# Expert loop in another order: the next expert's gate and up products ahead of the present expert's down products

## Chip, cores and metric

One NeuronCore of a Trainium2 chip runs the whole program. The metric is the device time of one execution in microseconds (us), median of the runs. All data is 32-bit float.

## What is computed

One step of a decoder of two layers over 512 prompt tokens and 32 sample tokens (544 in all). Each layer is an attention stage (latent attention in layer 0, sliding window in layer 1) followed by a mixture of experts: 32 experts, each token goes to 2 of them. Cut to what matters here:

```
def run_block(args):                      # rows of one expert, weights of that expert
    xb, e = args
    hid = jax.nn.silu(xb @ w_gate[e]) * (xb @ w_up[e])      # 1024 -> 512, twice
    return hid @ w_down[e]                                  # 512 -> 1024
...
yr = yr.astype(jnp.float32) * row_w[:, None]
y = jnp.zeros((n_tok, shape[-1]), jnp.float32).at[row_tok].add(yr)
```

The weights of an expert are three matrices of 2 MiB (gate, up, down), so 32 experts in two layers read 64 x 6 MiB from memory.

## The kernel before, in words

The kernel is written by hand for each engine; nothing plans the order, semaphores alone tie the engines together. `happened(name, k)` is "the event `name` has come k times", `landed` the same for a transfer. Each layer has a function `experts(L)` on every engine, with a loop over the 32 experts e; b is the parity of e (which of two buffers), s = (e + 2) % 3 the weight slot.

What one expert e does:

- TensorE (`expert`, L2320 to L2354): *gate and up*, 16 matmuls of 512 columns in pairs that share the array (64 columns of it each), from xeT[b] and the slot's gate and up weights into PSUM bank b, signal gu_mm; `fetched_T(e + 1)`, 8 transposes of the next expert's gathered rows (signal xt_mm); `numbers(e + LOOK)`, five small matmuls that give the row numbers of expert e + 3 (idx_mm); the wait for the hidden rows (hid_ready) and 4 transposes of them (ht_mm); the wait for hidT_ready, and *down*, 8 matmuls of 512 columns in pairs into bank 2 + b (d_mm).
- ScalarE (L974 to L983): after gu_mm, Silu from bank b; `rows_T(e + 1)`, the copy of the transposed rows to xeT; after d_mm, the copy of one half of the result to ye[b] (y0_ready).
- VectorE (L1575 to L1593): `mark(e + 3)`, the product silu x up (L1582, hid_ready), `numbers(e + 3)` (L1524, L1526), the copy of the transposed hidden rows to hidT (L1587), the copy of the other half of the result (L1593).
- GpSimd: gathers the rows of expert e + 3 from memory (L664), scatters the result rows of e (L674).
- SyncE issues the weight transfers (L495 to L500) and has three slots for them. Expert e's gate and up (L487) go out once gu_mm of e - 3 has come, its down (L492) once d_mm of e - 3 has come, strictly in this order on one queue.

In the trace all matmuls carry the line of the helper `mm` (L1923) and all transposes that of `flip` (L1928). The trace joins a run of matmuls that follow each other: "x48" is the 16 pieces of one expert's down and the 32 of the next one's gate and up (each 32-bit matmul shows as two pieces).

After the loop of layer 0 SyncE loads the projection weights of layer 1 (wqkv): 4 MiB after gate and up of expert 30 (L528), 2 MiB after its down (L530). After either loop the result rows are read back (L547).

Of the kernel before, what the change touches and what calls it, by code (L numbers as in the profile page):

```python
# [13 lines left out]
D = 1024  # L14
# [158 lines left out]
def build(nc, a, o):  # L173
    with ExitStack() as ctx:
# [556 lines left out]
        def _(act):  # L731
            start_counts(act, "scalar")

            def copy(out, in_):
                return act.activation(out, in_, ACT.Copy)  # L735
# [207 lines left out]
            def experts(L):  # L943
# [30 lines left out]
                with act.Fori(0, NE // 2) as i:  # L974
                    for b in range(2):
                        e = 2 * i + b
                        act.wait_ge(sig["gu_mm"], happened("gu_mm", NE * L + e + 1))
                        act.wait_ge(sig["hid_ready"], happened("hid_ready", NE * L + e))
                        act.activation(sg[BLK:2 * BLK, :], ps[0:BLK, b, :], ACT.Silu).then_inc(sig["silu_ready"], 1)  # L979
                        rows_T(e + 1, 1 - b)  # L980
                        act.wait_ge(sig["d_mm"], happened("d_mm", NE * L + e + 1))
                        act.wait_ge(sig[f"scattered{b}"], landed(f"scattered{b}", STORES * L + i + 1))
                        copy(ye[b][0:BLK, 0:FF], ps[0:BLK, 2 + b, :]).then_inc(sig["y0_ready"], 1)  # L983
# [124 lines left out]
        def _(v):  # L1108
# [358 lines left out]
            def experts(L):  # L1467
# [107 lines left out]
                with v.Fori(0, NE // 2) as i:  # L1575
                    for b in range(2):
                        e = 2 * i + b
                        v.wait_ge(sig["idx_mm"], happened("idx_mm", FETCHES * L + e + LOOK - 1))
                        mark(e + LOOK, 1 - b)
                        v.wait_ge(sig["silu_ready"], happened("silu_ready", NE * L + e + 1))  # L1580
                        v.wait_ge(sig["ht_mm"], happened("ht_mm", NE * L + e))
                        v.tensor_tensor(hid[0:BLK, :], sg[BLK:2 * BLK, :], ps[BLK:2 * BLK, b, :], ALU.mult  # L1582
                                        ).then_inc(sig["hid_ready"], 1)
                        numbers(e + LOOK, 1 - b)
                        v.wait_ge(sig["ht_mm"], happened("ht_mm", NE * L + e + 1))
                        v.wait_ge(sig["d_mm"], happened("d_mm", NE * L + e))
                        v.tensor_copy(hidT, ps[:, 6, 0:KF * BLK].rearrange("p (k t) -> p k t", k=KF)  # L1587
                                      ).then_inc(sig["hidT_ready"], 1)
                        v.wait_ge(sig[f"scattered{b}"], landed(f"scattered{b}", STORES * L + i + 1))
                        v.tensor_copy(store_at[b][0:BLK, :], store_rows[0:BLK, cols(e, 1)])  # L1590
                        v.drain()
                        v.wait_ge(sig["d_mm"], happened("d_mm", NE * L + e + 1))
                        v.tensor_copy(ye[b][0:BLK, FF:D], ps[BLK:2 * BLK, 2 + b, :]).then_inc(sig["y1_ready"], 1)  # L1593
# [325 lines left out]
        def _(pe):  # L1919
# [341 lines left out]
            def experts(L):  # L2261
# [58 lines left out]
                def expert(i, r):  # L2320

                    e, b, s = 6 * i + r, r % 2, (r + 2) % SLOTS
                    pair, turn = 3 * i + r // 2, LOADS[(r + 2) % SLOTS] * L + 2 * i + r // SLOTS + 1
# [11 lines left out]
                    fetched_T(e + 1, 1 - b, (odd if b == 0 else even) + pair + 1)  # L2335
# [7 lines left out]
                    last.then_inc(sig["ht_mm"], 1)  # L2343
# [12 lines left out]
                with pe.Fori(0, NE // 6) as i:  # L2356
                    for r in range(6):
                        expert(i, r)
                for r in range(NE % 6):
                    expert(NE // 6, r)  # L2360
# [340 lines left out]
```

## Time and profile before

| what | us |
|---|---|
| median of 3 runs | 1859.22 |
| lowest and highest run | 1856.38, 1862.15 |
| the profiled execution, its own time | 1855.08 |
| span of the profiled execution | 1853.4 |
| mean granted TensorE clock in it, share of full speed | 0.931 |

The profiled execution is 4.1 us below the median of the runs. The expert loop of layer 0 runs from about 517 to 1020 us of the span, that of layer 1 from about 1316 to 1819 us, so that the two loops are more than half of the time. All times in the rows are us from the start of the span.

### The profile page before, as it was taken

How to read it: one execution, taken by the hardware profiler on the slowest of the kernel's cores; microseconds unless marked ns; L12 is line 12 of the kernel's file. 1: busy time of each engine (PE TensorE's matmuls, PEld its weight loads, DVE VectorE, ACT ScalarE, POOL GpSimd, SP SyncE). 2: the span in 40 equal slices, each digit the busy share in tenths (PEclk: the TensorE clock that was granted, in tenths of full speed). 3: DMA queues.
4: the chain of work that ended last, by engine and by line, in shares of the span. 5: the costliest groups of instructions: out<-in, count | busy, mean ns of one | idle time of the engine just before them, and what ended most of it. 6: DMA issues, size and time to landing. Idle time of an engine off the chain costs nothing.

```text
span 1853.4 us, 27694 instructions
## 1 busy us (share of the span) xinstructions
PE 1672.0 (90%) x9306; PEld 874.9 (47%) x9307; DVE 541.4 (29%) x1490; ACT 420.5 (23%) x888; POOL 247.8 (13%) x348
## 2 busy tenths in 40 slices
PE   7899899999888989898889999899898989899885
PEld 5466666655544444444434445455443434344332
DVE  2333343322421111111111656764211111111113
ACT  2233344421111111111111224341011111111112
POOL 1231024400011111111111301000111111111110
PEclk9899899999888999998999999999798989898987
DMA  5252137744489999999998800122999999999973
GB/s 180 70 153 85 50 128 251 250 160 164 172 339 405 409 411 408 405 410 408 411 411 362 308 13 6 41 112 108 360 399 412 415 412 405 403 403 406 404 329 150
DMA packets 83342, 515.60 MB, mean 278 GB/s; under 512 B 22664, under 2 KB 41049, under 8 KB 56794
## 3 DMA queue, kind: packets, MB, share of 16 engines
q1 hardware_dynamic: 61962, 461.35, 62.7%
q0 software_dynamic: 21296, 53.15, 8.7%
q8 instruction: 50, 0.82, 0.2%
q14 instruction: 34, 0.28, 0.0%
HBM read 506.99 MB, written 26.52 MB: 288 GB/s over the span
## 4 chain that ended last, share of the span: by engine, by line
PE 76%; DMA 7%; issue 6%; DVE 6%; ACT 3%; DVEq 1%; SPq 0%; ACTq 0%; POOLq 0%
PE ps L1923 67%; PE ps L1928 9%; DMA mem<-in_moe_w_up 5%; DVE mem L1582 1%; ACT mem L979 1%; ACT mem L735 1%; DMA mem<-moe_rows_back 1%; DVE mem L1701 0%; DMA mem<-in_cache_mla 0%; DMA mem<-in_mla_w_a 0%; DMA moe_rows_back<-mem 0%; DVE mem L1293 0%; ACT mem L906 0%; ACT mem L909 0%; DVE mem L1672 0%
## 5 line engine op out<-in xcount | busy, mean ns | idle before, releaser
L1923 PE MATMUL ps<-mem 128*64 128x512 f32 (+13 forms) x7330 | 1433.9, 493 | 100.3 <-issue 49.7
L1923 PEld LDWEIGHTS ps<-mem 128*64 128x64 f32 (+4 forms) x7330 | 646.1, 150 | 797.3 <-issue 710.4
L735 ACT ACTIVATE mem<-ps 128x512 f32<-128x512 f32 (+3 forms) x370 | 205.8, 568 | 723.0 <-PE ps L1923 526.3
L1928 PE MATMUL ps<-mem 128*128 128x128 f32 (+1 forms) x1976 | 273.4, 280 | 73.6 <-DVE mem L1582 45.7
L1928 PEld LDWEIGHTS ps<-mem 128*128 128x128 f32 (+1 forms) x1976 | 233.8, 171 | 172.6 <-issue 149.5
L1582 DVE TENSOR_TENSOR mem<-mem,ps 64x512 f32<-64x512 f32 x64 | 44.2, 690 | 471.0 <-ACT mem L979 471.0
L664 POOL DMA_INDIRECT mem<-moe_rows_in,mem x68 | 63.3, 931 | 559.6 <-issue 541.4
L1593 DVE COPY mem<-ps 64x512 f32<-64x512 f32 x64 | 44.4, 693 | 312.3 <-PE ps L1923 312.3
L674 POOL DMA_INDIRECT moe_rows_back<-mem x64 | 59.2, 925 | 355.0 <-DVE mem L1593 347.8
L979 ACT ACT_TABLE_LOAD x32 | 41.1, 1283 | 231.8 <-PE ps L1923 231.8
L979 ACT ACTIVATE mem<-ps 64x512 f32<-64x512 f32 x64 | 37.7, 589 | 199.8 <-PE ps L1923 199.4
L1281 DVE COPY mem<-ps 128x512 f32<-128x512 f32 x64 | 44.2, 692 | 77.3 <-PE ps L1928 73.2
L625 POOL DMA_DIRECT2D mem<-in_cache_mla x96 | 51.5, 537 | 104.8 <-PE ps L1923 94.8
L605 POOL DMA_DIRECT2D mem<-in_cache_mla x64 | 34.7, 542 | 114.3 <-issue 114.3
L1019 ACT ACTIVATE mem<-mem 128x256 f32<-128x256 f32 (+1 forms) x64 | 30.3, 474 | 61.8 <-DVEq L1706 61.8
L646 POOL DMA_DIRECT2D moe_rows_in<-mem x10 | 5.4, 537 | 239.1 <-DVE mem L1409 239.1
L1587 DVE COPY mem<-ps 128x256 f32<-128x256 f32 x64 | 27.2, 425 | 24.6 <-PE ps L1928 20.4
L1701 DVE CUSTOM_DVE_ANT_0 mem<-ps,mem 128x256 f32<-128x256 f32 (+1 forms) x64 | 26.3, 448 | 27.2 <-PE ps L1923 25.1
L1517 DVE TENSOR_TENSOR mem<-mem 128x320 f32<-128x320 f32 x70 | 33.7, 481 | 1.5 <-issue 0.7
L850 ACT ACTIVATE mem<-mem 128x128 f32<-128x128 f32 (+3 forms) x32 | 18.0, 561 | 37.7 <-DVEq L1230 37.7
L1627 DVE SCALAR_TENSOR_TENSOR mem<-mem 128x1024 f32<-128x1024 f32 (+1 forms) x16 | 20.5, 1281 | 20.4 <-DMA mem<-moe_rows_back 19.6
L752 ACT ACTIVATE mem<-mem 128x1024 f32<-128x1024 f32 x10 | 10.6, 1057 | 65.7 <-DVEq L1374 53.6
(233 smaller groups left out, 459.8 us busy)
## 6 DMA issues: line engine op xcount, KB each, us to landing
mem<-in_moe_w_gate SPq DMA_DIRECT2D x64, 2048.0 KB, 17.8
mem<-in_moe_w_up SPq DMA_DIRECT2D x64, 2048.0 KB, 25.5
mem<-in_moe_w_down SPq DMA_DIRECT2D x64, 2048.0 KB, 23.5
mem<-in_cache_mla POOLq DMA_DIRECT2D x160, 160.0 KB, 4.5
mem<-in_cache_mla SPq DMA_DIRECT2D x96, 160.0 KB, 5.5
mem<-moe_rows_back SPq DMA_DIRECT2D x8, 1024.0 KB, 8.3
mem<-in_mla_wo SPq DMA_DIRECT2D x1, 4096.0 KB, 14.2
moe_rows_in<-mem POOLq DMA_DIRECT2D x8, 512.0 KB, 3.0
```

The costliest lines, as they stand in the source:

```text
L605: g.dma_start(pages_flat[par][:, bass.ds(j * ROW, ROW)], a["cache_mla"][0][bass.ds(page, 1)].rearrange("a p c -> p (a c)")).then_inc(sig[f ...
L625: g.dma_start(pages[b % 2][:, j, :], a["cache_mla"][0][bass.ds(at[n], 1)].rearrange("a p c -> p (a c)")).then_inc(sig[f"late_pages{b % 2}" ...
L664: g.indirect_dma_start(out=xe[b][0:BLK, :], out_offset=None, in_=rows_in, in_offset=bass.IndirectOffsetOnAxis(ap=fetch_at[b][0:BLK, 0:1].b ...
L674: g.indirect_dma_start(out=rows_back, out_offset=bass.IndirectOffsetOnAxis(ap=store_at[b][0:BLK, 0:1].bitcast(U32), axis=0), in_=ye[b][0:B ...
L735: return act.activation(out, in_, ACT.Copy)
L979: act.activation(sg[BLK:2 * BLK, :], ps[0:BLK, b, :], ACT.Silu).then_inc(sig["silu_ready"], 1)
L1281: v.tensor_copy(kT[t % 2][:, n], ps[:, bank, :].rearrange("p (g c) -> p g c", g=2)).then_inc(sig[f"tp_ev{bank}"], 1)
L1517: v.tensor_tensor(onehot[b], rankm[:, :, cols(q, 1)].broadcast_to([P, TILES, BLK]), slots.unsqueeze(1).broadcast_to([P, TILES, BLK]), ALU. ...
L1582: v.tensor_tensor(hid[0:BLK, :], sg[BLK:2 * BLK, :], ps[BLK:2 * BLK, b, :], ALU.mult).then_inc(sig["hid_ready"], 1)
L1593: v.tensor_copy(ye[b][0:BLK, FF:D], ps[BLK:2 * BLK, 2 + b, :]).then_inc(sig["y1_ready"], 1)
L1923: return pe.matmul(out, lhsT, rhs, start=start, stop=stop)
L1928: return pe.transpose(out, in_, ident[at:at + n, at:at + n])
```

## The change

The loop on TensorE, ScalarE and VectorE is turned by half an expert. TensorE did: gate and up(e), turns(e), down(e), where "turns" is the 8 transposes of the next rows, the small matmuls of `numbers`, the wait for the hidden rows and their 4 transposes. It now does: gate and up(e + 1), down(e), turns(e + 1); ahead of the loop stand gate and up(0) and turns(0), behind it down(31). ScalarE does silu(e + 1), the copy of half the result of e, `rows_T(e + 2)`. VectorE does the product of e + 1, the copy of the result of e, then `numbers(e + 4)` and the copy to hidT of e + 1. SyncE's and GpSimd's programs, the buffers, the slots and the number of instructions of each kind for an expert are as before. The diff, cut to its core:

```diff
 # ScalarE
+                def follow(i, b):
+                    e = 2 * i + b
+                    silu(e + 1, 1 - b)
+                    rows_back_0(e, i, b)
+                    rows_T(e + 2, b)
+
+                silu(0, 0)
+                rows_T(1, 1)
+                with act.Fori(0, NE // 2 - 1) as i:
+                    follow(i, 0)
+                    follow(i, 1)
+                follow(NE // 2 - 1, 0)
+                rows_back_0(NE - 1, NE // 2 - 1, 1)
 # VectorE
+                def hidden_T(e, b):
+                    numbers(e + LOOK, 1 - b)
+                    v.wait_ge(sig["ht_mm"], happened("ht_mm", NE * L + e + 1))
+                    v.wait_ge(sig["d_mm"], happened("d_mm", NE * L + e))
+                    v.tensor_copy(hidT, ps[:, 6, 0:KF * BLK].rearrange("p (k t) -> p k t", k=KF)
+                                  ).then_inc(sig["hidT_ready"], 1)
...
+                def follow(i, b):
+                    e = 2 * i + b
+                    hidden(e + 1, 1 - b)
+                    rows_back_1(e, i, b)
+                    hidden_T(e + 1, 1 - b)
+
+                hidden(0, 0)
+                hidden_T(0, 0)
+                with v.Fori(0, NE // 2 - 1) as i:
+                    follow(i, 0)
+                    follow(i, 1)
+                follow(NE // 2 - 1, 0)
+                rows_back_1(NE - 1, NE // 2 - 1, 1)
 # TensorE
-                def expert(i, r):
-
-                    e, b, s = 6 * i + r, r % 2, (r + 2) % SLOTS
...
+                def follow(i, r):
+
+                    gate_up(i, r + 1)
+                    down(i, r)
+                    turns(i, r + 1)
+
+                gate_up(0, 0)
+                turns(0, 0)
+                with pe.Fori(0, (NE - 1) // 6) as i:
                     for r in range(6):
-                        expert(i, r)
-                for r in range(NE % 6):
-                    expert(NE // 6, r)
+                        follow(i, r)
+                for r in range((NE - 1) % 6):
+                    follow((NE - 1) // 6, r)
+                down(NE // 6, (NE - 1) % 6)
```

`gate_up`, `turns` and `down` on TensorE are the three parts of the old `expert`, each with the waits it had; `silu`, `rows_back_0`, `hidden` and `rows_back_1` are the parts of the old bodies on the other two engines.

## Rows read from the trace of the kernel before

**Rows 1.** The page: busy time of each engine, and the chain that ended last, by engine.
```profile
PE 1672.0 (90%) x9306; PEld 874.9 (47%) x9307; DVE 541.4 (29%) x1490; ACT 420.5 (23%) x888; POOL 247.8 (13%) x348
PE 76%; DMA 7%; issue 6%; DVE 6%; ACT 3%; DVEq 1%; SPq 0%; ACTq 0%; POOLq 0%
```

**Rows 2.** Timeline, one expert: start, us, engine, line, instructions [idle before <-releaser].
```profile
641.64 10.52 PE L1923 MATMUL ps<-mem 128*64 128x512 f32 x48 [0.71 <-issue]
...
652.10 1.10 PE L1928 MATMUL ps<-mem 64*128 64x64 f32 x8
652.26 1.28 ACT L979 ACT_TABLE_LOAD   x1 [6.34 <-PE ps L1923]
...
653.12 0.74 PE L1923 MATMUL ps<-mem 128*64 x10
...
654.27 0.69 DVE L1582 TENSOR_TENSOR mem<-mem,ps 64x512 f32<-64x512 f32 x1 [7.84 <-ACT mem L979]
...
655.25 0.66 PE L1928 MATMUL ps<-mem 64*128 64x64 f32 x4 [1.39 <-DVE mem L1582]
...
656.63 12.21 PE L1923 MATMUL ps<-mem 128*64 128x512 f32 x48 [0.71 <-issue]
```

**Rows 3.** Busy time in three stretches; last three columns: granted clock, DMA share, GB/s.
```profile
548.77:902.36 353.59, 319.96 (x1610) 147.30 (x1611) 60.99 (x161) 56.29 (x81) 42.91 (x47) 0.92 1.01 408
641.70:652.00 10.30, 10.30 (x48) 3.94 (x48) 1.09 (x2) 0.59 (x1) 1.85 (x2) 1.00 1.00 395
656.70:660.00 3.30, 3.30 (x10) 1.24 (x12) 0.00 (x0) 0.00 (x0) 0.63 (x1) 0.57 1.03 437
```

**Rows 4.** Up transfers issued 528.82, 502.11, 546.34, 966.27, 1345.12, 1437.96, 1763.19: last number us to landing.
```profile
mem<-in_moe_w_up SPq DMA_DIRECT2D x1, 2048.0 KB, 12.9
mem<-in_moe_w_up SPq DMA_DIRECT2D x1, 2048.0 KB, 19.0
mem<-in_moe_w_up SPq DMA_DIRECT2D x1, 2048.0 KB, 14.7
mem<-in_moe_w_up SPq DMA_DIRECT2D x1, 2048.0 KB, 37.8
mem<-in_moe_w_up SPq DMA_DIRECT2D x1, 2048.0 KB, 14.4
mem<-in_moe_w_up SPq DMA_DIRECT2D x1, 2048.0 KB, 18.0
mem<-in_moe_w_up SPq DMA_DIRECT2D x1, 2048.0 KB, 39.5
```

**Rows 5.** Timeline, TensorE, layer 0: gate and up of expert 28.
```profile
957.06 8.78 PE L1923 MATMUL ps<-mem 128*64 128x512 f32 x32 [4.20 <-DMA mem<-in_moe_w_up]
```

**Rows 6.** Timeline, TensorE: down(0) with gate and up(1), in layer 0 and layer 1.
```profile
532.81 12.92 PE L1923 MATMUL ps<-mem 128*64 128x512 f32 x48 [0.71 <-issue]
...
1331.59 12.89 PE L1923 MATMUL ps<-mem 128*64 128x512 f32 x48 [0.71 <-issue]
```

**Rows 7.** Timeline, SyncE's queue, layer 0: down(1), down(3), and the last wqkv issue.
```profile
501.25 0.34 SPq L492 DMA_DIRECT2D mem<-in_moe_w_down  x1
...
538.90 0.35 SPq L492 DMA_DIRECT2D mem<-in_moe_w_down  x1
...
1006.62 0.34 SPq L530 DMA_DIRECT2D mem<-in_swa_wqkv  x1
```

**Rows 8.** Timeline, TensorE: the last two experts' matmuls, in layer 0 and layer 1.
```profile
1000.62 12.83 PE L1923 MATMUL ps<-mem 128*64 128x512 f32 x48 [0.71 <-issue]
...
1016.49 3.65 PE L1923 MATMUL ps<-mem 128*64 128x512 f32 x16 [0.71 <-issue]
...
1800.36 12.22 PE L1923 MATMUL ps<-mem 128*64 128x512 f32 x48 [0.74 <-issue]
...
1815.62 3.65 PE L1923 MATMUL ps<-mem 128*64 128x512 f32 x16 [0.71 <-issue]
```

**Rows 9.** Timeline, TensorE: the first products with wqkv in layer 1.
```profile
1036.45 7.13 PE L1923 MATMUL ps<-mem 128*128 128x512 f32 x16 [1.43 <-ACT mem L1004]
```

More of the change, by code:

```diff
@@ L973, in experts, with silu, rows_back_0 @@
                 copy(sg[0:BLK, :], ps[0:BLK, 5, :]).then_inc(sig["first_act"], 1)
[L974 to L983, printed above, removed]
+                def silu(e, b):
+                    act.wait_ge(sig["gu_mm"], happened("gu_mm", NE * L + e + 1))
+                    act.wait_ge(sig["hid_ready"], happened("hid_ready", NE * L + e))
+                    act.activation(sg[BLK:2 * BLK, :], ps[0:BLK, b, :], ACT.Silu).then_inc(sig["silu_ready"], 1)
+                def rows_back_0(e, i, b):
+                    act.wait_ge(sig["d_mm"], happened("d_mm", NE * L + e + 1))
+                    act.wait_ge(sig[f"scattered{b}"], landed(f"scattered{b}", STORES * L + i + 1))
+                    copy(ye[b][0:BLK, 0:FF], ps[0:BLK, 2 + b, :]).then_inc(sig["y0_ready"], 1)
+                def follow(i, b):
[10 more added lines that the diff above has]
+                rows_back_0(NE - 1, NE // 2 - 1, 1)
                 act.wait_ge(sig["lst_ready"], happened("lst_ready", L + 1))
@@ L1574, in experts @@
                 numbers(LOOK - 1, (LOOK - 1) % 2)
[L1575 to L1593, printed above, removed]
@@ new lines, in hidden @@
+                def hidden(e, b):
+                    v.wait_ge(sig["idx_mm"], happened("idx_mm", FETCHES * L + e + LOOK - 1))
+                    mark(e + LOOK, 1 - b)
+                    v.wait_ge(sig["silu_ready"], happened("silu_ready", NE * L + e + 1))
+                    v.wait_ge(sig["ht_mm"], happened("ht_mm", NE * L + e))
+                    v.tensor_tensor(hid[0:BLK, :], sg[BLK:2 * BLK, :], ps[BLK:2 * BLK, b, :], ALU.mult
+                                    ).then_inc(sig["hid_ready"], 1)
@@ L2333, in expert, with turns @@
                     last.then_inc(sig["gu_mm"], 1)
[L2335 removed]
+                def turns(i, r):
+                    e, b, _, _ = place(i, r)
+                    fetched_T(e + 1, 1 - b, (odd if b == 0 else even) + 3 * i + r // 2 + 1)
                     numbers(e + LOOK, 1 - b)
@@ L2343, in expert, with down @@
                     last.then_inc(sig["ht_mm"], 1)
+                def down(i, r):
+                    e, b, s, turn = place(i, r)
                     pe.wait_ge(sig[f"d{s}_in"], landed(f"d{s}_in", turn))
```

13 lines of the change are left out of this document (11 added, 2 removed).

## The prediction

> **What bounds the kernel now.** I read four views, in this order. First the page: TensorE is busy for 90% of the span, and the chain that ended last lies on it for 76% [rows 1]. Read alone, that says TensorE is the bound and each of its gaps costs time. Second, the timeline of one expert, to see what a gap is made of [rows 2]. The 48 pieces (down of one expert, gate and up of the next) take 10.52 us. Then come 8 transposes (1.10), the small matmuls (0.74), an idle 1.39 until VectorE's product (L1582), 4 transposes (0.66), an idle 0.71 for the copy to hidT, and the next 48 pieces. That is 4.5 us from 652.16 to 656.63 in which TensorE does little, and it pays for it again afterwards: the next 48 pieces take 12.21 us. The clock says why: it is 1.00 of full speed (2.4 GHz) through the first run, and 0.57 in the stretch just behind the gap, nearly all of it at the lower level of 1.2 GHz [rows 3]. So the gap costs some 4.5 us in every expert and 1.7 us of clock in every other one.
>
> Third, the same stretches' DMA columns: the share is 1.01 over 354 us of the loop, at 408 GB/s [rows 3]. The 16 DMA engines never rest while TensorE has its gaps. Two resources look full, so, fourth, I asked which one falls behind the other, by the issue and landing of single transfers [rows 4]. The up weights of expert 4 in layer 0 land at 546.34 + 14.7 = 561.0, those of expert 31 at 966.27 + 37.8 = 1004.1: 443.0 us for 27 experts, 16.41 us each. In layer 1 they land at 1359.5 and 1802.7: 443.2 us, 16.41 each. TensorE starts its 48 pieces 23 experts apart at 548.77 and 902.36, the ends of the stretch in [rows 3]: 353.6 / 23 = 15.37 us each. TensorE is 1 us per expert faster than the weights. It can be so for a while, because three slots are full at the start: the time from issue to landing grows from 14.7 to 37.8 us, and in the end it stands and waits, 4.20 us for the up weights of expert 28 [rows 5]. So the loop as a whole is bound by the weight transfers. Their start, their pace and what follows the last landing set its end; TensorE only shapes the edges.
>
> **The change part by part.**
>
> *The gap in every expert goes.* The silu and product chain (table load 1.28, Silu, product, done 2.8 us after gate and up) [rows 2] now lies beside the down products of the expert before, which are a third of 10.52 = 3.5 us, and beside 1.84 us of transposes and small matmuls. The 0.71 us for hidT lies beside the next gate and up. TensorE would need 10.52 + 1.10 + 0.74 + 0.66 = 13.0 us an expert. Taken at its word that is 15.37 - 13.0 = 2.4 us in 62 experts, 147 us. What is late next is the weights: at 16.41 us an expert TensorE reaches them some 7 experts in (it starts with three slots full and gains 3.4 us per expert) and waits from then on, 1.7 to 3.4 us an expert. In steady state the gain is zero. The Trainium skill, "Perfetto Trace Analysis", section "Matmul Optimizations", asks for matmuls back to back because the engine's power follows its use; by that rule the 147 us would come. The clock in the trace does follow, but the landings say that the time isn't TensorE's to give. Bounds for the pace of the transfers: it carries the same bytes in the same order on the same queues. Within this trace it was 16.07 us over experts 4 to 10 of layer 1 (1359.5 to 1437.96 + 18.0 = 1456.0) and 16.51 over experts 10 to 31 (to 1802.7) [rows 4]. I take the mean, 16.41, since nothing that the engines are asked for changes; the ends are worth -0.34 and +0.10 times 54 experts, -18 and +5 us.
>
> *The start of the transfers.* Everything up to turns(0) is as before, so gate and up of expert 3 go out at 528.4, and land, up last, at 528.82 + 12.9 = 541.7 [rows 4]. Down(3) waits for down(0). Before, down(0) was the first third of the run at 532.81, cold, and down(3) went out at 538.90, in time to follow without a hole [rows 6, 7]. Now gate and up(1) stand ahead of down(0). Both start without the 0.71 us for hidT, at 532.1, and take the same 12.92 us: down(0) ends at 545.0, down(3) goes out at 545.2, and gate and up of expert 4, queued behind its wait on SyncE (they were free to go since gate and up(1) ended), at 545.6, about when they went out before. The queue has run dry since 541.7, and one transfer of 2 MiB more is in the way of up(4). Its landing: 4 MiB into an empty queue took 13.3 us from the first issue (528.4 to 541.7), 2 MiB more at a third of 16.41 makes 18.8, so 564.0; by the three issued in a row before (down(1), gate(2), up(2): 501.25 to 502.11 + 19.0, 19.9 us) 565.1 [rows 4, 7]. Before it was 561.0. So the transfers run 3.0 to 4.1 us late from here; I take 3.5. In layer 1 the same sum gives 1330.9 + 12.9 + 0.2 = 1344.0, landing 1362.8 to 1363.9 against 1359.5 [rows 4, 6]: 3.3 to 4.4, I take 3.8. The next round doesn't add: down(1) ends near 558, 6 us ahead of the end of what is queued. Later, with TensorE waiting at gate and up(e + 1), down(e) stands behind that wait and with it the issue of down(e + 3); but down(e + 1) and the weights of e + 2 and e + 3's gate and up are still queued then, 12 MiB or over 30 us, so the queue doesn't run dry.
>
> *The end.* Before, down(30) ran while up(31) was still on its way: the last 48 pieces start at 1000.62 and 1800.36, the weights land at 1004.1 and 1802.7 [rows 4, 8]. Down(31) ends at 1020.14 and 1819.27, 16.0 and 16.6 us behind the landing. Now gate and up(31) must wait for the landing, and down(30) is behind them. From the landing on everything is what those rows show from the start of the 48 pieces: 12.83 or 12.22, the small work, 3.65, in all 19.52 or 18.91 us. So the end is 3.5 us (layer 0) and 2.3 us (layer 1) later relative to the landing. Whether the first pieces are cold: TensorE then has waited some 2 to 3 us behind 2.5 us of small work, and the nearest row (4.20 us of waiting, then 8.78 us for the 32 pieces, where two thirds of 10.52 are 7.0) is cold [rows 5]. I keep it cold; warm it is 1.7 us less in each layer. For layer 0 I take 3.2, the mean of the two durations (3.5 and 2.9).
>
> *Carried along.* The 2 MiB of wqkv behind down(30) went out at 1006.62 [rows 7] and will at about 1020. Even with 19.0 us to landing it is there by 1039, before the first products with it, at 1036.45 + 6.7 = 1043 [rows 4, 9]: nothing. ScalarE's table loads (16 a layer, some 17 now, for the peeled ends) and VectorE's reordered copies are covered by the down products; uncovered, a load would be 1.28 us. The gather of e + 3 is still asked for two experts ahead: nothing.
>
> *The sum.* 3.5 + 3.8 + 3.2 + 2.3 = 12.8 us on the profiled execution: 1855.1 + 12.8 = 1867.9. The median of the runs lies 4.1 us above that execution, so 1872.0 us. With all terms at their ends (3.0 + 3.3 + 1.2 + 0.6 = 8.1; 4.1 + 4.4 + 3.5 + 2.3 + 5 = 19.3) it is 1867 to 1879.
>
> **The rivals.**
>
> *A. TensorE is the bound.* Place: every expert; price: -147 us, 1712 us; it decides if the transfers deliver an expert in under 13 us. For it: 76% of the chain [rows 1]. Against it: 16.41 us in both layers, growing time to landing, waits at the end. The Trainium skill, "DMA: Bandwidth & Descriptors", section "Measured", has 425 GB/s for 16 MB; as an estimate that is 14.8 us an expert, which would still be over 13.
>
> *B. The transfers go faster.* TensorE's triggers come in a denser bundle (down(e + 3) and gate and up(e + 4) together), and if the queue then keeps the 16.07 us of the early rows through all 27 experts, the 18 us of the pace pay for the edges: 1872.0 - 18 = 1854 us, about 5 us below the median, or anything from there to no change if only part is kept. It decides at a pace of 16.17, where 13 us are paid. Against it: the 16.07 is of one layer's start only, and rows gathered and scattered take from the same engines.
>
> *C. Slower still.* A wait inside the loop delays issues after all (a scatter or gather that is waited for, or a second dry spell in the queue at experts 4 to 6), 2 to 5 us more a layer: 1876 to 1882.
>
> *D. The edges are hidden.* Engines that are ahead of the slowest one take up the dry spell, and the end is warm: only some 1 to 2 us of 13 is left, 1861.
>
> **How the numbers follow.** Forecast (slower by 8 to 19 us) 0.66, C 0.10, B 0.12, D 0.07, A 0.05. Within 0.3% (5.6 us, about what a measurement of this kernel can tell from no change) lie D and most of B: 0.17. Slower by more: 0.76. Faster by more: A and the edge of B, 0.07. The range leaves out A, the lower part of B and the far end of C: 1858 to 1882.
>
> **What would show it.** In the profile after: up(4) lands 3 to 4 us later than 561.0 and 1359.5; the pace from there is 16.4; TensorE waits for up weights from about expert 7 in every expert, and its busy share falls although it has no other gap; down(31) ends 18.9 to 19.5 us behind the landing of up(31). The prediction is wrong if the landings come closer together than 16.2 us, if TensorE shows no waits for weights, or if the loops end at or before 1020 and 1819.

## The result and the profile after

The changed kernel takes 1863.16 us (median of 11 runs, 1859.74 to 1871.26), the kernel before beside it 1857.29 us (median of 11, 1855.6 to 1862.15). The ratio is 1.0035, 95% interval [1.0021, 1.0048]: slower by some 6 us, where the forecast's sum gave 12.8. The direction is right; the size is not, and the time lies in the stated range only because that range reached down to 1858 for the rivals B and D. The profiled execution took 1860.62 us, its span is 1858.9 against 1853.4 us of before.

The page of the changed kernel: busy time of each engine, the chain that ended last by engine, and the costliest group with its idle time (its releaser and the share of it stand last).

```profile
PE 1677.4 (90%) x9306; PEld 841.0 (45%) x9307; DVE 542.4 (29%) x1490; ACT 381.6 (21%) x858; POOL 247.3 (13%) x348
...
PE 52%; DMA 37%; DVE 5%; ACT 2%; issue 2%; SPq 1%; DVEq 1%; ACTq 0%; POOLq 0%
...
L1959 PE MATMUL ps<-mem 128*64 128x512 f32 (+13 forms) x7330 | 1441.7, 496 | 147.2 <-DMA mem<-in_moe_w_up 97.8
```

TensorE's share is still 90%, but the chain went from 76% on TensorE and 7% on the DMAs [rows 1] to 52% and 37%, and 97.8 us of TensorE's idle time end with an up transfer. The same bound now stands in the open: before, it was hidden behind gaps of TensorE's own. Note one more number: ScalarE has 858 instructions and 381.6 us where it had 888 and 420.5 [rows 1]. It will matter.

The same two stretches of the loops, first of the changed kernel, then of the one before (columns as in [rows 3]), and what TensorE waits for in layer 0 of the changed kernel, 560 to 1000 (us in total, times, longest):

```profile
560.00:960.00 400.00, 353.14 (x1744) 145.12 (x1742) 67.42 (x175) 44.41 (x75) 46.21 (x50) 0.90 1.01 408
1360.00:1760.00 400.00, 357.86 (x1748) 146.16 (x1745) 67.42 (x175) 44.41 (x75) 46.67 (x51) 0.88 1.01 407
```

```profile
560.00:960.00 400.00, 357.46 (x1791) 163.01 (x1792) 68.94 (x182) 62.29 (x91) 48.15 (x52) 0.92 1.01 408
1360.00:1760.00 400.00, 359.46 (x1790) 162.51 (x1792) 70.17 (x182) 61.07 (x90) 48.15 (x52) 0.92 1.01 408
```

```profile
PE ps L1959 <- DMA mem<-in_moe_w_up: 51.7, 25, 3.7
```

The DMA share is the same to the last digit, and so are the 408 GB/s but for 407 in layer 1. TensorE does the same work with another kind of rest: 25 waits for weights in layer 0, up to 3.7 us each, the first at 594.86, that is at expert 6, the last at 990.05, at expert 30. The pace comes from four transfers, up of experts 4 and 31 in either layer, issued at 542.14, 969.5, 1344.6 and 1773.8:

```profile
mem<-in_moe_w_up SPq DMA_DIRECT2D x1, 2048.0 KB, 19.5
mem<-in_moe_w_up SPq DMA_DIRECT2D x1, 2048.0 KB, 35.5
mem<-in_moe_w_up SPq DMA_DIRECT2D x1, 2048.0 KB, 19.7
mem<-in_moe_w_up SPq DMA_DIRECT2D x1, 2048.0 KB, 33.7
```

They land at 561.6, 1005.0, 1364.3 and 1807.5: 443.4 and 443.2 us for 27 experts, 16.42 and 16.41 each, as before the change. So the pace didn't move, and the difference is in what lies around it. To measure that I use two intervals in every kernel below: the *start*, from the issue of up(3) to the landing of up(30), and the *end*, from there to the end of down(31). The start holds the beginning of the queue and the 27 experts behind it, 81 transfers; since the pace is nearly the same, it shows what the beginning costs. (Over the kernels with full traffic and recorded landings the pace from up(4) to up(31) is 16.34 to 16.44 us an expert, so a difference of 1 or 2 us between two single traces is weak.) Up(30) is the last transfer at which TensorE surely waits after the change. (The traces of e1 to e4 below hold no landing of the weights; there the start of TensorE's run behind its wait stands for it, which in the changed kernel is 0.05 us later.)

| us | start, layer 0 | start, layer 1 | end, layer 0 | end, layer 1 | down(31) to issue of up(3) in layer 1 |
|---|---|---|---|---|---|
| before | 459.9 | 459.8 | 31.4 | 31.9 | 307.5 |
| after | 461.1 | 462.6 | 32.1 | 32.45 | 307.5 |

The four differences are +1.2, +2.8, +0.7 and +0.55: 5.3 of the 5.5 us by which the spans differ. The forecast had 3.5 + 3.8 + 3.2 + 2.3.

How far the queue runs dry at the beginning can be read in the 10 us that begin 12 us behind the issue of up(3). In layer 1, the changed kernel and the one before (last three columns: clock, DMA share, GB/s):

```profile
1341.65:1351.65 10.00, 10.00 (x60) 4.64 (x58) 1.93 (x6) 1.19 (x2) 1.87 (x2) 1.00 0.75 275
1339.62:1349.62 10.00, 9.29 (x56) 4.60 (x54) 1.56 (x5) 1.19 (x2) 1.61 (x2) 1.00 0.94 358
```

The loop has 408, so the changed kernel misses 1.3 MB there, 3.3 us of transfers. The one before already misses 1.2 us. In layer 0 it is 338 and 349 GB/s.

The start, in TensorE's timeline of the changed kernel (layer 0, then layer 1), and in SyncE's queue in layer 0:

```profile
528.18 1.09 PE L1964 MATMUL ps<-mem 64*128 64x64 f32 x8
529.21 0.74 PE L1959 MATMUL ps<-mem 128*64 128x2 f32 x10
529.92 0.66 PE L1964 MATMUL ps<-mem 64*128 64x64 f32 x4
530.55 10.52 PE L1959 MATMUL ps<-mem 128*64 128x512 f32 x48
...
1331.29 12.22 PE L1959 MATMUL ps<-mem 128*64 128x512 f32 x48
```

```profile
541.11 0.35 SPq L492 DMA_DIRECT2D mem<-in_moe_w_down  x1
541.70 0.34 SPq L487 DMA_DIRECT2D mem<-in_moe_w_gate  x1
```

The reader is to see what is missing: there is no idle time ahead of the four transposes of turns(0), although nothing but the next rows lies between gate and up(0) and them. The forecast had this piece "as before", with its idle of 1.4 us. And the 48 pieces that follow take 10.52 us in layer 0, where the forecast kept 12.92 [rows 6]. Down(0) ends at 541.1 and not at 545.0. Why is in ScalarE's timeline:

```profile
514.59 1.28 ACT L978 ACT_TABLE_LOAD   x1
```

That is the only load of layer 0; there is one more, at 1313.78, where the loop before had 32. The first Silu used to stand inside the hardware loop and now stands ahead of it; its load moved ahead of it too, and ahead of the wait for gate and up(0), and the loads inside the loop are gone with it. So the change as measured is two things at once, another order and 30 table loads fewer.

The end, in TensorE's timeline of the changed kernel:

```profile
990.05 12.22 PE L1959 MATMUL ps<-mem 128*64 128x512 f32 x48 [2.23 <-DMA mem<-in_moe_w_up]
...
1004.95 10.52 PE L1959 MATMUL ps<-mem 128*64 128x512 f32 x48 [0.37 <-DMA mem<-in_moe_w_up]
...
1018.50 3.65 PE L1959 MATMUL ps<-mem 128*64 128x512 f32 x16 [0.71 <-issue]
...
1807.52 10.52 PE L1959 MATMUL ps<-mem 128*64 128x512 f32 x48 [0.71 <-DMA mem<-in_moe_w_up]
```

The last run of 48 pieces starts with the landing of up(31), as forecast, but behind only 0.37 and 0.71 us of idle time, and it is warm (all of it at the full clock): 10.52 us in both layers. A run that begins at the lower clock and takes longer is called cold here. The forecast had it cold (12.83, 12.22).

### The profile page after: what moved, and what is told of

The parts are those of the page before. It is cut to its first block, busy times and chain, and to the rows that moved or that the text cites. A ratio compares the mean times of both kernels' runs of the same rounds, so it can differ in the third digit from the quotient of the medians.

```text
span 1858.9 us, 27654 instructions
## 1 busy us (share of the span) xinstructions
PE 1677.4 (90%) x9306; PEld 841.0 (45%) x9307; DVE 542.4 (29%) x1490; ACT 381.6 (21%) x858; POOL 247.3 (13%) x348
## 4 chain that ended last, share of the span: by engine, by line
PE 52%; DMA 37%; DVE 5%; ACT 2%; issue 2%; SPq 1%; DVEq 1%; ACTq 0%; POOLq 0%
PE ps L1959 45%; DMA mem<-in_moe_w_up 34%; PE ps L1964 6%; ACT mem L735 1%; DMA mem<-in_cache_mla 1%; DMA mem<-moe_rows_back 1%; DMA mem<-in_mla_w_a 0%; DVE mem L1737 0%; SPq L487 0%; DMA moe_rows_back<-mem 0%; SPq L445 0%; SPq L492 0%; DVE mem L1309 0%; ACT mem L906 0%; ACT mem L909 0%
## 5 line engine op out<-in xcount | busy, mean ns | idle before, releaser
L1959 PE MATMUL ps<-mem 128*64 128x512 f32 (+13 forms) x7330 | 1441.7, 496 | 147.2 <-DMA mem<-in_moe_w_up 97.8
L1959 PEld LDWEIGHTS ps<-mem 128*64 128x64 f32 (+4 forms) x7330 | 611.9, 150 | 885.1 <-issue 707.3
L1540 DVE TENSOR_SCALAR mem<-ps 64x1 f32 (+1 forms) x70 | 10.5, 150 | 74.0 <-PE ps L1959 73.9
L726 POOL TENSOR_TENSOR mem<-mem 128x1024 f32<-128x1024 f32 (+1 forms) x5 | 12.3, 2471 | 91.7 <-PE ps L1964 91.6
```

Source lines behind the costliest of these rows:

```text
L1959: return pe.matmul(out, lhsT, rhs, start=start, stop=stop)
```

## The experiments

The theory after this comparison: the loops are bound by the transfers; the order costs at the start, because down(3) is asked for late and keeps gate and up(4) behind it on SyncE; it costs little at the end; and it gains on a side that no one meant, the table load. The first rival: the order costs nothing at the start and the difference is in the end alone. The second: TensorE bounds the loop after all, and the removed loads hide it.

### e1: down(0) in its old place

```diff
 # TensorE (ScalarE and VectorE alike)
+                down(0, 0)
+                gate_up(0, 1)
+                turns(0, 1)
-                with pe.Fori(0, (NE - 1) // 6) as i:
-                    for r in range(6):
+                with pe.Fori(0, (NE - 2) // 6) as i:
+                    for r in range(1, 7):
                         follow(i, r)
-                for r in range((NE - 1) % 6):
-                    follow((NE - 1) // 6, r)
```

> The changed kernel with one difference: down(0) stands ahead of gate and up(1) as in the kernel before, and the loop is turned from expert 1 on. Theory T (the transfers bind the loop, the change only costs at its two edges): the 0.6 and 2.7 us that the transfers run late at up(4) go, so 5.9 - 3.3 = 2.6 us over the kernel before, and the time from the landing of up(31) to the end of down(31) stays 17.2 us. Rival R (the loss arises in the loop, from two transfers issued in one bundle and deeper queues): no change, 5.9 us over the kernel before. The forecast's own start term (7.3 us) would put it below the kernel before, at -1.4 us.

Measured: 1859.61 us (12 runs), ratio to before 1.0016 [1.0005, 1.0027], +3.0 us. The start is 460.2 and 459.7 us, as in the kernel before. In its queue down(3) is issued 7.6 us behind up(3) (12.2 in the changed kernel):

```profile
533.43 0.38 SPq L487 DMA_DIRECT2D mem<-in_moe_w_up  x1
541.03 0.35 SPq L492 DMA_DIRECT2D mem<-in_moe_w_down  x1
```

The place of one down product out of 32 is worth about 3 us of 6, the start's share (the two intervals just overlap, so the size of this 3 is rough). The queue doesn't run dry any more: 422 and 410 GB/s in the 10 us where the changed kernel has 338 and 275. The mechanism of the start holds, at 4.0 of the forecast's 7.3 us. The profiled execution of e1 is 8.0 us longer than that of before, but 4.6 of this stand ahead of the issue of up(3) in layer 0 (533.43 against 528.82), where the edit hasn't acted yet, and its last runs in layer 1 were cold (end 34.6). One span is a weaker witness than the two intervals and the median.

### e2: down(30) in its old place

```diff
 # TensorE (ScalarE and VectorE alike)
-                for r in range((NE - 1) % 6):
-                    follow((NE - 1) // 6, r)
+                down(NE // 6, (NE - 2) % 6)
+                gate_up(NE // 6, (NE - 1) % 6)
+                turns(NE // 6, (NE - 1) % 6)
```

> The changed kernel with one difference: down(30) stands ahead of gate and up(31), as in the kernel before; the loop is turned from expert 0 to 30. Theory T: down(30) runs while up(31) is on its way, so 1.1 and 0.6 us go (the ends at full clock as the changed kernel's trace has them): 5.9 - 1.7 = 4.2 us over the kernel before. With the cold end that was forecast, 5.5 us would go: 0.4 us over it. Rival R: no change, 5.9 us.

Measured: 1865.12 us (7 runs), 1.0046 [1.0029, 1.0063], +8.5 us, where the theory had 4.2 and its rival 5.9. The end is 32.5 us in both layers, no better than after (32.1, 32.45). Its last runs:

```profile
992.34 12.21 PE L1963 MATMUL ps<-mem 128*64 128x512 f32 x48 [2.29 <-DMA mem<-in_moe_w_up]
...
1007.59 10.52 PE L1963 MATMUL ps<-mem 128*64 128x512 f32 x48 [0.71 <-issue]
...
1021.15 3.65 PE L1963 MATMUL ps<-mem 128*64 128x512 f32 x16 [0.71 <-issue]
```

TensorE no longer waits for up(31): from the start of gate and up(30) it has 12.21 + 2.5 of small work + 0.71, and at 1007.59 up(31) is there. In the changed kernel up(31) lands 14.9 and 15.2 us behind up(30), not 16.4, so TensorE's own work binds from up(30) on in e2, and all but 0.37 and 0.71 us of it after the change. The forecast tied the loss to the landing of up(31) and to down(30) behind it. It is tied to up(30): down(29) still stands behind that landing, where the kernel before had started the run with down(29) at 985.59, 3.1 us ahead of it. Putting one product back at the very end therefore returns nothing.

The start of e2 is worth a look too, since nothing in it differs from the changed kernel there: 462.8 and 462.6 us. Its first run of 48 pieces took 12.22 us in layer 0, where the changed kernel's took 10.52 and had 461.1. So 1.7 us of layer 0's start is the clock in that one run.

### e3 and e9: SyncE's order turned too

```diff
 # SyncE
-                def follow(e, s):
+                def next_gate_up(e, s):
                     sp.wait_ge(sig["gu_mm"], happened("gu_mm", NE * L + e - 2))
                     gate_up(e, s)
+
+                def next_down(e, s):
                     sp.wait_ge(sig["d_mm"], happened("d_mm", NE * L + e - 2))
                     down(e, s)
...
+                next_gate_up(SLOTS, 2)
                 with sp.Fori(0, 9) as i:
                     for r in range(SLOTS):
-                        follow(SLOTS * (i + 1) + r, (r + 2) % SLOTS)
+                        next_gate_up(SLOTS * (i + 1) + r + 1, r)
+                        next_down(SLOTS * (i + 1) + r, (r + 2) % SLOTS)
...
+                next_gate_up(NE - 1, (NE + 1) % SLOTS)
+                next_down(NE - 2, NE % SLOTS)
+                next_down(NE - 1, (NE + 1) % SLOTS)
```

> The changed kernel with SyncE's order turned as well: gate and up of e + 1 are issued ahead of down of e, from expert 3 on, each still behind the same count. Theory T: up(4) no longer stands behind the wait for down(0), so the queue doesn't run dry at the start (0.6 and 2.7 us back), and up(31) lands two transfers (11 us) ahead of the end of the transfers, where it landed one (5.4 us) ahead; down(31) then ends 6 to 9 us sooner in each layer than in the changed kernel. Time 9 to 13 us under the kernel before. The pace of the transfers stays 16.4 us an expert. Rival R: the pace changes with the order of the bundle; the time stays within 3 us of the changed kernel. If TensorE were the bound: no change.

Measured: 1854.68 us (12 runs), 0.9993 [0.998, 1.0006], 2.0 us under before (not clear of no difference) and 8 under the changed kernel. The start interval falls to 453.7 and 454.9 us, 5 to 6 under before. Most of that isn't the beginning of the queue: in the turned order up(30) stands ahead of down(29), so the interval holds 80 transfers and not 81, and one is worth 16.41 / 3 = 5.5 us. What is left is -0.7 and +0.6 on before, where the changed kernel has +1.2 and +2.8: the beginning costs nothing any more. The queue shows that; gate and up(4) go out 9.6 us behind up(3) (13.2 in the changed kernel), ahead of down(3):

```profile
528.96 0.44 SPq L487 DMA_DIRECT2D mem<-in_moe_w_up  x1
538.09 0.35 SPq L487 DMA_DIRECT2D mem<-in_moe_w_gate  x1
538.54 0.38 SPq L487 DMA_DIRECT2D mem<-in_moe_w_up  x1
541.51 0.34 SPq L492 DMA_DIRECT2D mem<-in_moe_w_down  x1
```

and the 10 us from 12 us behind up(3) are full:

```profile
540.96:550.96 10.00, 10.00 (x60) 4.68 (x60) 1.81 (x5) 1.42 (x3) 1.87 (x2) 1.00 1.00 422
```

The 5.5 us are the gain at the other side: up(31) too lands one transfer sooner relative to the last one, down(31). The profiled span, 1846.7, is further under before than the median, so e9 is the same program once more:

> The same program as e3_sp_order, once more beside the kernel before. In e3 the trace and the median did not say the same: the profiled span was 12 us under the changed kernel's, the median of the runs only 8 us. If the gain is the shorter start (up(30) lands 454 to 455 us after the issue of up(3), against 459.8 before) and part of it is given back in the stage between the layers in most executions, the median is again 1853 to 1856 us, ratio 0.998 to 1.000, and the trace shows 453 to 456 us again in both layers. If the profiled execution of e3 was the rule and its median disturbed, the median is 1848 to 1850 us (ratio 0.996). If e3's start was chance, up(30) lands 461 us after the issue of up(3) and the time is 1862 us.

Measured: 1853.23 us (12 runs), 0.9985 [0.9972, 0.9998], 3.0 us under before. The start interval is 453.6 and 454.7, so that is no chance. But the ends are 34.0 and 34.1 us (+2.6, +2.2 on before), and the way from down(31) to up(3) of layer 1 is 310.5 (+3.0; 310.7 in e3). The last two experts, layer 0:

```profile
981.20 10.52 PE L1965 MATMUL ps<-mem 128*64 128x512 f32 x48 [1.39 <-DMA mem<-in_moe_w_up]
996.15 12.22 PE L1965 MATMUL ps<-mem 128*64 128x512 f32 x48 [2.11 <-DMA mem<-in_moe_w_up]
```

This is the end that the forecast described: behind a wait of 2.11 us the last run is cold, and down(31) ends 18.9 us behind the landing of up(31). Only the order of warm and cold differs from the changed kernel. In both kernels warm runs (10.52) and cold ones (11.9 to 13.5) follow each other irregularly in the loop. Which kind is the last isn't tied to the order of the products, since e3, the very same program, had a warm last run in both layers (10.52) and in layer 1 an end of 32.4 us against 34.1 in e9. So some 1.7 us of each end are chance of the phase.

Behind the loop the rows are read back 8.6 us after down(31) in e9 and 8.9 in e3, against 6.0 before and 6.2 after, and the next stage has a gap of some 4.5 us:

```profile
1023.62 9.69 SPq L553 DMA_DIRECT2D mem<-moe_rows_back  x5
...
1031.37 1.94 PE L1970 MATMUL ps<-mem 128*128 128x128 f32 x8 [4.46 <-issue]
```

That the last scatter is slowed by the weights of the next stage, which now start earlier, is my reading; no run tested it. For it: in layer 1, where no such weights follow, the read-back comes 5.6 (e3) and 5.9 us (e9) behind down(31). Against it: e8 below has the same order on SyncE and reads back after 5.9 us in layer 0. From the read-back to the issue of up(3) in layer 1 the stage takes 301.3 us in the changed kernel, 301.6 and 301.8 here, but 303.8 in e2, 303.9 in e4 and 304.0 in e7, whose edits don't touch it. So 2 to 3 us between the layers come and go without an edit.

### e8: SyncE's order turned in the kernel before

The same edit as e3, on TensorE's old order.

> The kernel before, on TensorE, ScalarE and VectorE, with SyncE's order turned as in e3 (gate and up of e + 1 issued ahead of down of e). Theory T: with the old order of the products the issue of down stands behind gate and up(e + 1), which come 7 us after it; the queue runs dry for 4 us at the start, and at the end down(30) is waited for first: 2 to 8 us slower than the kernel before. Rival (SyncE's order alone brings what e3 has over the changed kernel): 4 us or more faster than the kernel before.

Measured: 1872.41 us (6 runs), 1.0101 [1.0073, 1.013], +16.9 us, more than either theory had. Both halves of the first theory are in the trace. At the beginning gate and up(4) go out late, at 544.84, with down(3) right behind, and the queue is empty for 3 us (no byte between 541.9 and 544.9): in the 10 us from 12 us behind up(3) it has 176 and, in layer 1, 141 GB/s, against 349 and 358 before.

```profile
540.31:550.31 10.00, 9.29 (x57) 4.56 (x55) 1.56 (x5) 1.19 (x2) 1.10 (x2) 1.00 0.53 176
1347.74:1357.74 10.00, 9.29 (x56) 4.55 (x54) 1.56 (x5) 1.19 (x2) 1.87 (x2) 1.00 0.45 141
```

The start interval hides it: 458.2 and 459.5 us look no longer than before, but they hold one transfer less, as in e3. Against 459.9 - 5.5 and 459.8 - 5.5 they are 3.8 and 5.2 us longer. The end is 39.5 and 39.7 us, against 31.4 and 31.9; of these 8 us, 5.5 are the same shift of up(30), and 2.6 and 2.3 are new. TensorE waits for down weights; first the waits in layer 0 from 560 to 1030 (us in total, times, longest), then the last 48 pieces:

```profile
PE ps L1929 <- DMA mem<-in_moe_w_down: 17.1, 10, 2.3
```

```profile
1007.15 12.09 PE L1929 MATMUL ps<-mem 128*64 128x512 f32 x48 [1.03 <-DMA mem<-in_moe_w_down]
```

Up(31) lands at 1001.4, but TensorE wants down(30) first, and that now stands behind gate and up(31) in the queue. It starts both 5.7 us after up(31) is there, where the old order has done down(30) by then. In all 14 us in the two loops and 2.2 between them. The same edit is worth -8 us on one order and +17 on the other: the order of the queue must be TensorE's.

### e10: both

The changed kernel with the edits of e1 and e3.

> The changed kernel with both edits: down(0) ahead of gate and up(1), as e1, and SyncE's turned order, as e3. If e1's gain (3 us) is only that down(3) goes out early enough, it can't come on top of e3's: with the turned order on SyncE down(3) waits behind gate and up(4), which want the end of the same run of products, so the time is e3's, 1853 to 1856 us, up(30) 454 to 456 us after the issue of up(3). If the two gains are of separate causes and add up, it is 1850 to 1852 us with 452 to 453 us. The rival for which it loses: before's TensorE order at the start with SyncE's turned order has the dry spell of e8_before_sp_order, 1 to 3 us longer than e3's, 1856 to 1858 us.

Measured: 1859.62 us (12 runs), 1.001 [0.9994, 1.0026], +3.4 us beside before by the medians, 1.9 by the ratio. The gains don't add. Gate and up(4) now wait for the end of a run that starts with down(0), and go out 14.8 us behind up(3) (544.96 and 530.20):

```profile
530.20 0.44 SPq L487 DMA_DIRECT2D mem<-in_moe_w_up  x1
544.96 0.36 SPq L487 DMA_DIRECT2D mem<-in_moe_w_gate  x1
```

This is e8's dry spell on the turned order, as the third of the expectations had it: the start intervals, 458.4 and 457.7 us, hold 80 transfers like e3's and are 4.8 and 3.0 us longer than e9's. The ends are 33.8 and 34.3 us (a cold last run, as in e9), the way between the layers 313.5 (+6.0): 2.8 of it ahead of the read-back, as in e9, and 3.2 behind it, in the stage that varies by 2 to 3 us anyhow. The median is above the 1856 to 1858 us expected, but the interval of the ratio holds them; it doesn't hold the 1850 to 1852 us of gains that add.

Rate of the transfers in the 10 us from 12 us behind the issue of up(3), all kernels with full traffic:

| GB/s | layer 0 | layer 1 |
|---|---|---|
| before | 349 | 358 |
| after, e2 | 338, 265 | 275, 277 |
| e1, down(0) in its old place | 422 | 410 |
| e3, e9, both orders turned | 422, 413 | 420, 399 |
| e8, only SyncE's order turned | 176 | 141 |
| e10 | 246 | 253 |
| e4, the load put back | 205 | 164 |
| e5, before without its loads | 413 | 426 |

### e4: the table load back in its old place

```diff
 # ScalarE, ahead of the first Silu
+                act.wait_ge(sig["gu_mm"], happened("gu_mm", NE * L + 1))
+                turnstile(act)
```

> The changed kernel with one difference: ScalarE's table load for the first Silu comes behind gate and up(0) again (it had moved ahead of the wait when that Silu left the loop). Theory T: this is why the start cost less than forecast (3.3 us against 7.3 us): TensorE waits some 1.4 us for the hidden rows of expert 0 again and gate and up(1) with down(0) run partly at the lower clock, down(0) ends 2 to 4 us later and the transfers start later by as much: 1 to 4 us more than the changed kernel in all, 7 to 10 us over the kernel before. Rival (the load has nothing to do with it, the clock at the start is chance): as the changed kernel, 5.9 us.

Measured: 1871.81 us (6 runs), 1.008 [1.0058, 1.0102], +15.2 us, some 9 above the changed kernel; yet the edit puts back only one load a layer. Layer 0:

```profile
529.10 1.28 ACT L978 ACT_TABLE_LOAD   x1 [13.87 <-PE ps L1961]
...
532.00 0.67 PE L1966 MATMUL ps<-mem 64*128 64x64 f32 x4 [1.39 <-DVE mem L1599]
```

This is the idle of 1.39 us that the forecast took for given. TensorE's 48 pieces then take 12.22 us, and the start becomes 464.3 and 464.1, +4.4 and +4.3 on before. With the load in place the start term comes out at or a little above the forecast's 3.5 and 3.8: its working was right for a condition that the change removed. By spans it is 10.7 us above the changed kernel: 3.2 and 1.5 at the starts, 1.3 and 1.9 at the ends (down(31) takes 5.00 and 5.35 us instead of 3.65), 2.4 between the layers and 0.7 ahead of up(3). Beside before its loops are 4.4 + 4.3 at the starts and 2.0 + 2.5 at the ends longer, 13.2 us, and its median of 1871.81 is the forecast's 1872.0. At the starts that is the forecast's mechanism; at the ends it is luck, since the last run of 48 pieces was warm (10.52) and down(31) was slow instead. Beside e2, whose first run of layer 0 was cold as well (462.8), the idle of 1.39 us alone is worth 1.5 us at the start. The edit moves one load a layer and costs more than its 1.28 us, because what it delays is an issue of transfers and not TensorE alone.

### e5: the kernel before without its 32 table loads

```diff
 # ScalarE, ahead of the loop
+                act.activation(lt[0:1, 94:95], eps[0:1, 0:1], ACT.Silu)
```

A Silu of one number ahead of the loop; nothing reads its result, and all else is the kernel before.

> The kernel before with one Silu of a single number put ahead of ScalarE's loop, so that the loop holds no table load. Theory T (transfers bind): TensorE's gap is 1.3 us shorter in every other expert and its clock stays high, which moves nothing but the first experts; between -3 and +1 us, up weights still land 16.4 us apart and TensorE waits for them from an earlier expert on. Rival (TensorE's gaps were worth their time): 32 x 1.28 = 41 us faster, up to 95 with the clock.

Measured: 1851.29 us (12 runs, 1849.34 to 1853.59), 0.9977 [0.9962, 0.9991], 4.2 us under before: the lowest median of the complete kernels (the intervals of e3 and e9 overlap with it). Start 457.2 and 457.7 (-2.7, -2.1). The rival, that TensorE is the bound and an idle of 1.39 us less per expert brings 41 to 95 us, is out. Timeline of its first experts and the windows of both loops:

```profile
529.63 0.67 PE L1929 MATMUL ps<-mem 64*128 64x64 f32 x4 [0.23 <-issue]
531.01 10.52 PE L1924 MATMUL ps<-mem 128*64 128x512 f32 x48 [0.71 <-issue]
```

```profile
560.00:960.00 400.00, 350.01 (x1796) 152.24 (x1793) 67.38 (x177) 45.30 (x77) 47.20 (x51) 0.96 1.01 408
1360.00:1760.00 400.00, 355.62 (x1799) 155.29 (x1800) 69.23 (x180) 45.04 (x76) 48.13 (x52) 0.94 1.01 408
```

One turn further in, the transposes that follow gate and up, and VectorE's product:

```profile
650.62 1.10 PE L1929 MATMUL ps<-mem 64*128 64x64 f32 x8
...
651.35 0.69 DVE L1583 TENSOR_TENSOR mem<-mem,ps 64x512 f32<-64x512 f32 x1 [6.40 <-ACT mem L980]
```

The product starts 0.73 us behind the transposes' start, with the load it was 2.17 [rows 2]. The idle of 1.39 us is gone, the 48 pieces are warm, the clock is 0.96 and 0.94 (0.92 before), and still 408 GB/s. Faster TensorE, same pace, 4 us at the edges. At the beginning down(3) and gate and up(4) are asked for in time, so the queue stays full (413 and 426 GB/s in the table above). If the two parts add, the change splits into some -4 us for the loads and some +10 for the order. In the profiled executions both are larger, since the ends of e5 are 30.8 and 29.1 us: its two loops are 8.1 us shorter than before, and those of the changed kernel 13.4 longer than e5's; 4.1 us of the gain are lost in the stage between the layers.

TensorE's own need can be read here too. Until it first waits for weights, its runs start at 531.01, 544.57, 558.28 and so on to 653.73: 13.6 us an expert in the old order without loads.

### e6 and e7: both kernels with a third of the weight traffic left out

```diff
 # SyncE, for experts 3 to 31
-                    gate_up(e, s)
+                    gate_up(e, s, KD * FF // 2)
...
```

> The kernel before with a third of the weight traffic left out: from expert 3 on only the first half of every partition's gate and up weights is loaded (1 MiB each), down in full; the products run on what the slot holds. Its outputs are not the reference's. Theory T: 4 MiB are 10.9 us, so TensorE binds at its own 15.1 us an expert: 31 x 15.1 = 468 us from gate and up(0) to down(31) where it was 492, 48 us in both layers: about 1809 us.

> The changed kernel with the same third of the weight traffic left out (gate and up in halves from expert 3 on; outputs not the reference's). Theory T: 10.9 us of transfers are under TensorE's 12.8 us an expert, so the turned loop brings what was held back: 31 x 12.8 = 397 us a layer, about 1667 us, 142 us under the kernel before with the same traffic. Rival R (the turned order has a hidden wait of its own): over 13.5 us an expert, over 1700 us.

Measured: before's order 1844.36 us (6 runs), the changed kernel 1678.77 us (2 runs). Beside the kernel before with its full traffic that is 0.9934 [0.9911, 0.9956] and 0.9046 [0.901, 0.9083]. The same stretch, 560 to 900, of the one and of the other:

```profile
560.00:900.00 340.00, 307.06 (x1544) 142.27 (x1544) 59.33 (x157) 54.04 (x79) 40.74 (x44) 0.92 0.80 291
```

```profile
560.00:900.00 340.00, 340.00 (x1868) 147.09 (x1864) 71.68 (x185) 47.71 (x81) 48.06 (x52) 1.00 0.95 351
```

With the transfers out of the way (DMA share 0.80) before's TensorE has its gaps and its clock of 0.92; the turned order is busy for 340.00 of 340 us at 1.00. Its runs of 48 follow each other without an idle time, 12.77 us apart (645.44, 658.21, 670.98); over 13.5, as the rival for e7 had it, is out, and the time is 12 us above the theory's 1667.

The old kernel needs 15.2 us (runs start at 701.84, 716.97 and 732.22). So the change is worth 2.4 us an expert and 166 us in all where the weights arrive in time, and less than nothing where they don't. But the change is the order and the loads together, and by e5's 13.6 us most of the 2.4 belongs to the loads and the clock that they cost: 15.2 to 13.6 without them, 13.6 to 12.8 by the order. No run has the old order without loads at the lighter traffic, so this split is worked out, not measured.

My expectation for e6, 1809 us, was 35 us low: it gave each loop 24 us, and between the first run (532.46) and down(31) (1008.11) e6 takes 475.7 us where before takes 483.7 (532.81 to 1016.49), 8 less. Only 11 us come free in all, although 1.2 us an expert lie between 15.2 and 16.4. The reason is that before's TensorE worked through its store of weights for most of the loop and waited for up weights for 5.4 us in layer 0 (560 to 1000) and 3.6 in layer 1 (1360 to 1800), no more. Before the change both bounds end within a few us of each other; that is what makes either one look like the bound.

## Why the prediction came out as it did

- *The loop is bound by the weights, not by TensorE*: right, though by a thin margin: with a third of the traffic left out the kernel before gains only 11 us (e6). The pace is 16.42 and 16.41 us (forecast 16.41), the waits begin at expert 6, the seventh, as forecast, rival A (-147 us) didn't happen, and e6 and e7 show those very 2.4 us an expert once the transfers are lighter. The Trainium skill, "Perfetto Trace Analysis", section "Matmul Optimizations", wants matmuls back to back. The trace of e7 has that, with 1.00 of the clock, and e7 takes 166 us less than e6; the changed kernel doesn't get it, because from expert 6 on it waits for weights in every expert.
- *The gap of 4.5 us in every expert* was a misreading. It holds for every second one, where a table load and with it the idle 1.39 us falls (15 waits, 21.4 us, in layer 0 from 560 to 1000); in the others the gap is 3.1 us (1013.38 to 1016.49 in [rows 8]). Had the text asked why every second one, it would have met the load.
- *Rival B, a faster pace*: out. Neither layer's mean moved by more than 0.01 us. *Rival C*, a second dry spell or wait, is out with it.
- *The start, 3.5 and 3.8*: this step failed in its premise. "Everything up to turns(0) is as before" was wrong for ScalarE: the table load moved ahead of the loop. That took 1.6 us off the idle time and let layer 0's run go warm (10.52 for 12.92; the warm run isn't sure, in e2 it took 12.22 with the load out of the way), so down(3) went out at 541.1 instead of 545.2 and up(4) landed at 561.6 instead of 564.0 to 565.1. Measured +1.2 in layer 0; in layer 1, where the run took 12.22, +2.8. e4 puts the load back and finds 4.4 and 4.3; e1 puts down(0) back and finds 0.3 and -0.1. The mechanism (down(3) late, gate and up(4) behind it) is shown, the condition was wrong. The text costed these loads at nothing ("covered by the down products") and priced only the uncovered case as a loss; that the edit could take them out of the loop wasn't considered. ScalarE's sum was made from the diff's instructions, and the load isn't one of them.
- *The end, 3.2 and 2.3*: this step failed as well. It took the whole of a down product (less the clock) as added behind the landing of up(31). Measured against that landing it is 17.15 and 17.2 us behind 16.07 and 16.57, +1.1 and +0.65. The run was warm, 10.52 for 12.83 and 12.22, and these 2.3 and 1.7 us are the whole of what was too much. The text named this alternative ("warm it is 1.7 us less in each layer") and chose the wrong end; e9, with the last run cold, shows +2.6 and +2.2. The forecast had set the cold run by a row with 4.20 us of waiting, and there were 0.37 and 0.71. It also tied the term to the wrong landing: up(31) lands only 15 us after up(30), and by e2 TensorE's own work from up(30) on would make the end as late.
- *Carried along, nothing*: right for wqkv, wrong for the table loads (forecast some 17 a layer, measured 1). The second part of wqkv went out at 1015.5, the first products with it start 16.5 us behind down(31), 16.3 before.
- *Rival D, edges hidden, 1861*, is where the time came closest: of the 12.8 us, 5.3 were left. But its reason (engines ahead take up the dry spell) isn't what the runs show for the start.

The sum by its terms: forecast 3.5 + 3.8 + 3.2 + 2.3 = 12.8; measured 1.2 + 2.8 + 0.7 + 0.55 = 5.3.

## What to carry to other kernels

When a loop is turned on the engine that computes, turn the issue order of its transfers with it, at the first issues and the last: the same edit on SyncE was worth -8 us in the turned order and +17 in the old one. When you compare intervals between two transfers, count the transfers in them: with SyncE's order turned there is one less, 5.5 us, and that hid a dry spell of 4 to 5 us in e8. Before reordering for an engine's sake, cut the traffic of its rival: the pair e6 and e7 shows what the change could be worth (166 us) and e5 what a faster engine brings today (4 us). And when the first use of an activation function crosses the edge of a hardware loop, count its table loads before and after: here one stray instruction ahead of the loop does more for the time than the whole reordering.

## What the runs showed of the hardware

- ScalarE's table load for Silu, 1.28 us, came 32 times with Silu inside the hardware loop and 2 times with one Silu ahead of it. Where it is issued behind a wait it lies on the path; with no instruction of that function waiting in front of it, it was done 12.4 us early (514.59 + 1.28, first Silu at 528.31). Without it the product comes 1.44 us earlier (0.73 for 2.17). The Trainium skill, "ScalarE: Activation LUTs", section "What ACT_TABLE_LOAD costs", gives 1283 ns for the load and 1380 ns of drain on top of it for a switch. The trace of before agrees with the first (1283 ns, mean of 32); the second doesn't show in these 1.44 us.
- The 16 DMA engines gave 406 to 410 GB/s in every loop with full traffic, whatever the order of issue. With lighter traffic the share fell to 0.80 at 291 GB/s and stood at 0.95 at 351 GB/s, so what they moved for a given share was less than in the full loops (364 and 369 GB/s for a share of 1).
- TensorE's granted clock is lower in the changed kernel's loops, which wait for weights, than in before's, with gaps of its own (0.90 and 0.88 against 0.92; 1.00 in e7, which never rests). Waiting for weights alone isn't the mark: e5 does it too, with 0.96 and 0.94. The same 48 pieces take 10.52 to 13.5 us. In the middle of the loop that costs nothing, since the pace stays; at the first and the last expert it is 1.7 us.
